# Delta rule, first third: gate columns in split passes, one table set for exponential and logarithm, decays and key products moved

## The reference, cut to what matters

```python
proj = h @ w_in                                   # 4096 columns qkv and z, 8 of b, 8 of a
qkv, z, b_raw, a_raw = split(proj)
qkv = silu(causal_dwconv(qkv, conv_w))            # width 4
q = l2norm(q) * GDN_HEAD_DIM ** -0.5;  k = l2norm(k)
beta = sigmoid(b_raw)
g = -exp(a_log) * softplus(a_raw + dt_bias)       # log decay, per head and token
g = cumsum(g, axis=-1)                            # within a chunk
decay = exp(where(causal, g[..., :, None] - g[..., None, :], -inf))
m = where(strict, einsum("bhnid,bhnjd->bhnij", k * beta, k) * decay, 0.0)
u = triangular_solve(I + m, v * beta)             # and w likewise; then the scan over chunks
```

## Time and profile before

| what | us |
|---|---|
| median of three runs | 1367.81 (1364.25 to 1372.63) |
| profiled execution | 1367.86 |
| its span, first to last instruction | 1366.1 |
| PE busy in the span | 1314.6 (96%) |
| PE from the first matmul of `begin` to the start of tile 13 | 590.80 to 672.03 |
| mean granted TensorE clock | 0.978 of 2.4 GHz |

### The profile page before, as it was taken

How to read it: one execution, slowest core, us unless ns; L and a number is a source line. 1 busy time by engine, 2 the same in 40 slices (tenths; PEclk the granted TensorE clock), 3 DMA queues, 4 the chain that set the end, 5 groups by cost and what they waited for, 6 DMA issues and landing times.

```text
span 1366.1 us, 28690 instructions
## 1 busy us (share of the span) xinstructions
PE 1314.6 (96%) x10343; PEld 1249.7 (91%) x10343; DVE 736.7 (54%) x1539; ACT 706.8 (52%) x1233; POOL 879.3 (64%) x366
## 2 busy tenths in 40 slices
PE   8899989999999999999999999999999999999997
PEld 3589889999989999978989998999999999999996
DVE  4879984321466664254735424655552676555632
ACT  3554445354455555467323224766665555666653
POOL 0454667478859888844222223788888786888794
PEclk9999989999999999998899899999999999999998
DMA  8964436245536555733211211555556554555562
GB/s 336 346 229 161 155 126 210 97 154 183 177 122 205 180 182 169 194 121 110 70 54 63 66 59 64 171 183 181 171 168 188 175 182 154 187 184 179 168 181 74
DMA packets 60837, 217.75 MB, mean 159 GB/s; under 512 B 9832, under 2 KB 11112, under 8 KB 57936
## 3 DMA queue, kind: packets, MB, share of 16 engines
q1 hardware_dynamic: 60752, 216.56, 49.0%
HBM read 215.48 MB, written 1.05 MB: 159 GB/s over the span
## 4 chain that ended last, share of the span: by engine, by line
issue 45%; POOL 38%; PE 15%; ACT 1%; POOLq 1%; DVE 1%; ACTq 0%; DVEq 0%
POOL w_lo L561 38%; PE bank L653 9%; PE bank L732 5%; POOLq L558 0%; ACT h L1410 0%; POOLq L560 0%; ACT w_hi L1410 0%; PE bank L591 0%; PE bank L776 0%; PE bank L592 0%; PE bank L596 0%; ACT bank L1410 0%; DVE bank L3109 0%; POOLq L561 0%; DVE bank L3194 0%
## 5 line engine op out<-in xcount | busy, mean ns | idle before, releaser
L561 POOL TENSOR_TENSOR w_lo<-w_raw,w_hi 128x1024 fp32r<-128x1024 f32 x356 | 876.2, 2472 | 469.6 <-ACT w_hi L1410 468.6
L1410 ACT ACTIVATE w_hi<-w_raw 128x1024 fp32r<-128x1024 f32 x356 | 375.1, 1057 | 142.4 <-PE bank L732 50.6
L653 PE MATMUL bank<-a_hi,w_hi 128*128 128x256 f32 (+4 forms) x1032 | 293.4, 284 | 1.0 <-POOL w_lo L561 1.0
L653 PE MATMUL bank<-a_hi,w_lo 128*128 128x256 f32 (+4 forms) x1032 | 293.0, 284 | 0.0
L653 PE MATMUL bank<-a_lo,w_hi 128*128 128x256 f32 (+4 forms) x1032 | 292.8, 284 | 0.0
L630 PE MATMUL bank<-a_hi,w_hi 128*128 128x256 f32 (+3 forms) x752 | 226.2, 301 | 4.7 <-DVE a_lo L2275 3.9
L630 PE MATMUL bank<-a_lo,w_hi 128*128 128x256 f32 (+3 forms) x752 | 222.4, 296 | 0.0
L630 PE MATMUL bank<-a_hi,w_lo 128*128 128x256 f32 (+3 forms) x752 | 222.1, 295 | 0.0
L653 PEld LDWEIGHTS bank<-a_hi,w_hi 128*128 128x128 f32 x1032 | 195.8, 190 | 1.5 <-POOL w_lo L561 1.2
L653 PEld LDWEIGHTS bank<-a_lo,w_hi 128*128 128x128 f32 x1032 | 195.8, 190 | 0.1
L653 PEld LDWEIGHTS bank<-a_hi,w_lo 128*128 128x128 f32 x1032 | 195.9, 190 | 0.0
(11 more groups left out here) (442 smaller groups left out, 2572.9 us busy)
## 6 DMA issues: line engine op xcount, KB each, us to landing
w_raw<-in_s SPq DMA_DIRECT2D x284, 512.0 KB, 3.5
w_raw<-in_down SPq DMA_DIRECT2D x48, 512.0 KB, 3.5
adaw<-in_w_ada SPq DMA_DIRECT2D x16, 1024.0 KB, 7.4
w_raw<-in_down SPq DMA_DIRECT2D x24, 384.0 KB, 3.1
adab<-in_w_ada_first SPq DMA_DIRECT2D x4, 2048.0 KB, 9.2
ctxt<-in_ctx SPq DMA_DIRECT2D x1, 1024.0 KB, 11.1
x<-in_x SPq DMA_DIRECT2D x1, 1024.0 KB, 17.5
out_h<-h SPq DMA_DIRECT2D x4, 256.0 KB, 2.6
```

The costliest lines, as they stand in the source:

```text
L561: pool.tensor_tensor(w_lo[:, s], w_raw[:, s], w_hi[:, s].bitcast(F32), ALU.subtract) \
L653: ins = mm(banks[bank][:, tk], w_[:, s, k], x_[:, k, tk], start=(m == 0), stop=(m == 3 * KD - 1))
L1410: return nc.scalar.activation(out_, in_, f, **kw)
```

## The change

The gate columns `wba` get a rounded and a low half (ACT, then POOL), and `ba(k)` becomes three fp32r matmuls. ACT preloads the table set that holds exponential and logarithm, and does the gates' absolute value, exponential and logarithm in one run; tanh comes later, under Silu's set. Taps 2 and 3 move behind `rows_ready`; the decay exponentials move from behind the squares of tile 5 to behind `rounded(8)`. DVE runs both key products without taps between them. PE does `y(1, 1)` ahead of fI2. `claimed` waits for each bank of a stage just before the heads that go into it.

```diff
+        wba_hi, wba_lo = (at(f"wba_{n}", [P, KD, 40], where_, F32R) for n, where_ in
+                          (("hi", small_at[0]), ("lo", small_at[0] + 1280)))
...
+        STAGES.remove(("fI2", (6, 7)))
+        STAGES.insert(STAGES.index(("y1.1", (4,))) + 1, ("fI2", (6, 7)))
... POOL
-            remainders(0, UNITS)
+            a_in_ahead = UNIT0["a_in"] + SLOTS
+            remainders(0, a_in_ahead)
+            pool.wait_ge(wba_rounded, 1)
+            pool.tensor_tensor(wba_lo[:], wba[:], wba_hi[:].bitcast(F32), ALU.subtract).then_inc(wba_split, 1)
+            remainders(a_in_ahead, UNITS)
... PE
+            def claimed(name, cols, rows):
+                for (heads, dst), b in zip(heads_in(name, cols, rows), BANKS[name]):
+                    if TURN[name, b]:
+                        pe.wait_ge(taken[b], TURN[name, b])
+                    yield heads, dst
... in broadcast_g, products, by_token, flip, turned, new_values, state_update, w_t, chunk_outputs
-                claim(name)
-                for heads, dst in heads_in(name, cn, cn):
+                for heads, dst in claimed(name, cn, cn):
...
             def ba(k):
-                ins = mm(banks[5][0:40, 0:N2], wba[:, k], h[:, k], start=(k == 0), stop=(k == KD - 1))
+                if k == 0:
+                    pe.wait_ge(wba_split, 1)
+                for m, (w_, x_) in enumerate(((wba_hi, a2_hi), (wba_lo, a2_hi), (wba_hi, a2_lo))):
+                    ins = mm(banks[5][0:40, 0:N2], w_[:, k], x_[:, k, 0:N2], start=(k == 0 and m == 0), stop=(k == KD - 1 and m == 2))
...
             a_in(12, 13)
+            y(1, 1)
             pe.wait_ge(mt_scaled, 4)
             flip("fI2", 2, "uu")
-            y(1, 1)
             y(2, 1)
... ACT
             root(RMS_END, N1, 0)
+            act.wait_ge(gdn_in, 112)
+            fn(wba_hi[:], wba[:], ACT.Copy).then_inc(wba_rounded, 1)
             act.wait_ge(h_in, 16)
...
-            nc.scalar.preload_act_table(ACT.Silu)
+            nc.scalar.preload_act_table_set("natural_log_exp_and_others")
             tap3(0)
-            rounded(0)
...
-            link(fn(tok[:, 0], banks[5][32:32 + HN, 0:N2], ACT.Tanh, scale=0.5))
-            fn(tok[:, 5], banks[5][0:HN, 0:N2], ACT.Abs, bias=hb[:, 1:2]).then_inc(abs_ready, 1)
-            fn(tok[:, 0], tok[:, 0], ACT.Identity, bias=1.0)
+            fn(tok[:, 0], banks[5][32:32 + HN, 0:N2], ACT.Copy)
+            link(fn(tok[:, 5], banks[5][0:HN, 0:N2], ACT.Abs, bias=hb[:, 1:2]))
+            act.sem_inc(abs_ready, 1)
+            link(fn(tok[:, 5], tok[:, 5], ACT.Exp, scale=-1.0))
             fn(hb[:, 2:3], hb[:, 0:1], ACT.Exp)
-            act.wait_ge(abs_ready, 1)
-            link(fn(tok[:, 5], tok[:, 5], ACT.Exp, scale=-1.0))
+            fn(tok[:, 5], tok[:, 5], ACT.Ln, bias=1.0).then_inc(log1p_ready, 1)
+            rounded(0)
             tap3(1)
             rounded(1)
... the copies to halves
-            fn(tok[:, 5], tok[:, 5], ACT.Ln, bias=1.0).then_inc(log1p_ready, 1)
-            tap3(2)
-            rounded(2)
-            nc.scalar.preload_act_table(ACT.Exp)
-            tap3(3)
-            rounded(3)
... the rows of the decays, up to glsp
+            tap3(2)
+            rounded(2)
+            tap3(3)
+            rounded(3)
             nc.scalar.preload_act_table(ACT.Silu)
...
             rounded(4)
+            link(fn(tok[:, 0], tok[:, 0], ACT.Tanh, scale=0.5))
+            fn(tok[:, 0], tok[:, 0], ACT.Identity, bias=1.0)
             prefill(1)
...
             squared(5)
+            tap3(7); rounded(7); activated(6); squared(6); activated(7); squared(7)
+            tap3(8); rounded(8)
             nc.scalar.preload_act_table(ACT.Exp)
             for n, c in enumerate((1, 2, 0)):
                 decay(c, n + 1)
             nc.scalar.preload_act_table(ACT.Silu)
-            tap3(7); rounded(7); activated(6); squared(6)
-            tap3(8); rounded(8); activated(7); squared(7)
...
             rounded(11)
+            flipped("fI1", 1, "tt")
+            product_out(2, 3)
             activated(10)
             squared(10)
-            flipped("fI1", 1, "tt")
-            product_out(2, 3)
... DVE
-            v.tensor_scalar(raw, raw, hb[:, 1:2], 0.0, ALU.add, ALU.max)
-            taps(1)
+            link(v.tensor_scalar(raw, raw, hb[:, 1:2], 0.0, ALU.add, ALU.max))
... the running sum, up to gcum_ready
-            taps(2, 3, 4)
+            taps(1, 2, 3)
... the token columns of rows
             differences(1)
-            taps(5)
+            taps(4, 5)
             differences(2)
...
             key_products(1, 1, 2)
-            taps(10)
             key_products(2, 2, 3)
-            taps(11)
             flipped("fI1", 1, "tt")
-            taps(12)
+            taps(10, 11, 12)
             flipped("fI2", 2, "tt")
```

More of the change, by code:

```diff
@@ L312, in bass_two_blocks @@
             "centre_done conv_seq act_done glu_done g_rounded g_ready")
-        conv_evac, conv4_seq, conv4_act, wba_clear = sems("conv_evac conv4_seq conv4_act wba_clear")
+        conv_evac, conv4_seq, conv4_act, wba_clear, wba_rounded, wba_split = sems(
+            "conv_evac conv4_seq conv4_act wba_clear wba_rounded wba_split")
         abs_ready, log1p_ready, gcum_ready, rows_ready = sems(
@@ L1058, in broadcast_g @@
                 c0, cn = CHUNKS[c]
-                claim(f"g{c}")
-                for heads, dst in heads_in(f"g{c}", cn, cn):
+                for heads, dst in claimed(f"g{c}", cn, cn):
                     for i in range(dst.shape[1]):
@@ L1078, in by_token @@
                 c0, cn = CHUNKS[c]
-                claim(name)
-                for heads, dst in heads_in(name, P, cn):
+                for heads, dst in claimed(name, P, cn):
                     for i in range(dst.shape[1]):
@@ L1139, in turned @@
                     return
-                claim(name)
-                for heads, dst in heads_in(name, GC, GC):
+                for heads, dst in claimed(name, GC, GC):
                     for i in range(4):
@@ L1176, in state_update @@
                 read_out(f"kt{c}")
-                claim(name)
-                for heads, dst in heads_in(name, P, P):
+                for heads, dst in claimed(name, P, P):
                     for i in range(4):
@@ L1188, in w_t @@
                 read_out(f"kt{c}")
-                claim(name)
-                for heads, dst in heads_in(name, cn, P):
+                for heads, dst in claimed(name, cn, P):
                     for i in range(4):
@@ L1848, in _ @@
             squared(5)
+            tap3(7)
+            rounded(7)
+            activated(6)
+            squared(6)
+            activated(7)
+            squared(7)
+            tap3(8)
+            rounded(8)
             nc.scalar.preload_act_table(ACT.Exp)
@@ L1852, in _ @@
             nc.scalar.preload_act_table(ACT.Silu)
[L1853 to L1860, removed]
             tap3(9)
```

1 line of the change is left out of this document (added).

## The result

The changed kernel takes 1357.05 us (median of 6, 1354.67 to 1362.36) where the kernel before takes 1366.94 (median of 6, 1364.25 to 1372.63). The ratio is 0.9922, 95% interval 0.9893 to 0.9950. The profiled execution took 1354.67 with a span of 1352.8. The forecast was 1356.

What follows compares the result with a forecast made beforehand. TensorE alone was taken as the bound, losing 17.9 us to idle time and half clock between `begin` and tile 13. Columns 3.0, waits 3.8 and clock 4.7 gave 11.5 off 1367.86: 1356.4, said as 1356, range 1346 to 1363.

Steps and rivals of the forecast that it cites:

- Gate columns: In `begin`: a step falls from 1.53 to 1.16 us, eight steps save 3.0 us; bounds 0 and 6.1.
- wba_hi and wba_lo: Ahead of `ba(0)`: the copy on ACT and subtraction on POOL cost 0, with 1.1 us of cover.
- Gates: Token rows behind `begin`: ready near 606.5, TensorE comes at 609.3, so the 3.9 us wait goes with 2.8 to spare.
- Squares and decays: At hk: `squared(7)` ends near 626, hk is reached at 629, so the 1.7 us wait goes.
- Key products: From hk to the y pair: new waits 3.9 us in place of 7.7, 2.8 of them at fI2's VectorE half; gain 3.8.
- `claimed`: At kk2's second bank: four heads may start earlier; gain bounded by 0 and 0.8 us, taken as 0.
- Clock: Half-clock stretches between `begin` and tile 13: loss falls from 10.2 to 5.5 us, gain 4.7; bounds 0 and 10.2.
- the clock gives nothing back: Rival: all three half-clock stretches return, gain only 6.8 us, time 1361; chance 0.15.
- it decides: Rival: no half-clock stretch falls, gain 17.0 us, time 1351, or 1347 if the one at 757.37 goes too; chance 0.25.
- The slower rival: From near y(2, 1) up to tile 17 the clock stays low, some 36 us at half, 18 lost: 1370.6; chance 0.06.
- The table set: Rival, in the gate rows: the set does not hold, three loads return, rows 1.1 us late, 1359; chance 0.04.

Runs made afterwards that it cites:

- the run with the gap put back: The changed kernel with the old order of the gates on ACT and DVE (three more table loads, taps 2 and 3 ahead of the rows): 1365.37 us, ratio 0.9981.
- the run with g2 twice: The changed kernel with each of the eight 8-row matmuls of g2 done once more into the same place: 1360.55 us, ratio 0.9946.

## Why the prediction was right, and where it was not

**The sum was right, its split was not.** It had 6.8 us for columns and waits and 4.7 for the clock. On the averages the span is 10.8 us shorter, of which 9.2 ± 0.5 is rest and 1.6 ± 1.1 is loss. That 1356 came so close is luck: one term was 2.4 too small and the other 3.1 too large. Either error alone would have left the time inside the stated range.

*Gate columns.* Predicted 1.16 us a step and 3.0 in all; measured 1.12 to 1.14 and 12.24 - 9.38 = 2.9. Undoing them cost 2.8 without clock. The nearest rows, the fp32r matmuls beside them, were the right price. By the count of four passes in the Trainium skill, FP8 and Floating Point Precision, section TensorE Precision Notes, the gain would have been about 1 (an estimate from that count and the row's 0.59): here the float32 matmul cost 0.59 and 0.22 to its follower, the three split ones 0.37 and 0.12, so about half of the gain is outside the product itself. What the prediction did not say is that this term depends on another: alone, with the gates in their old order, 0.4 of it is spent at once as a longer wait, and no change of the time was measured in two sets, though the rest fell by 2.0 ± 0.4.

*wba_hi and wba_lo.* Cost 0, as predicted, but the cover was thinner: POOL's subtraction took 1.04 us, not 0.75, and ended at 591.27. `ba(0)` came at 592.31, 0.6 later than before, which kept 1.04 of cover; at the old 591.72 it would have been 0.45. The estimate divided a unit's time by its columns, and the measured time of the shorter one is above that share.

*Gates.* Predicted ready near 606.5 and asked for at 609.3; measured 607.04 and 609.73. The wait is gone with 2.7 to spare. The thinnest cover held too, at half its size: unit 4 is subtracted at 603.87 + 2.39 = 606.3, predicted 605.4, and tile 4 starts near 606.7. Undone, this part costs 8.3 us, the most of the three parts that were undone.

*Squares and decays.* No wait at hk, as predicted; it stays away with the gates' order undone and with the products' order undone. That it was this move that took it is by elimination, no run shows it alone.

*Key products.* Predicted 0.3 + 0.3 + 0.5 + 2.8 = 3.9 of waits, measured 0.2 at the first y group and 2.2 at the second, 2.4. The place, the releaser and the cause of the new wait were right, VectorE's chain a little faster than its group means say. The old waits were 7.7 and the 0.3 ahead of the y pair in the earlier trace rows, which the prediction left out of that sum, so like for like 8.0 - 2.4 = 5.6 are gone, not 3.8. That is what the waits at the token rows and at hk had been; the other old waits, 2.4, have made room for 2.4 of new ones. With the key products in their old order the waits come to 1.9, so this part's own order took none away.

*`claimed`.* The prediction put it at 0, bounded by the 0.8 of kk2. It missed a wait further on: in the transposes of `kr` TensorE waited 0.78 us in all four profiles with the old `claim` and waits 0.25 in all ten with `claimed`, whichever other part is undone. That is 0.5 us. No run undoes `claimed` alone, but starting four heads before the second bank is free is what it does. 2.9 + 5.6 + 0.5 = 9.0, which fits the 9.2 of rest.

*Clock.* This is the term that was mis-sized: 4.7 predicted, 1.6 ± 1.1 on the averages. The profiled execution alone seems to say otherwise. In the changed stage 20.5 us at half clock became 6.8, so 3.4 were lost and not 5.5, and the stretch in the g stage that was kept for g2 did not come; behind 740 it lost 6.8 against 5.1. The table of 14 profiles shows what went wrong. The side of the changed kernel was forecast well: 3.4 us at half clock in the g stage and 7.6 near the y pair, where the profiles without the old gap and those with the new wait have 3.4 and 6.3 on the mean. The side of the kernel before was taken from one execution, 20.5 us, with a stretch at 665.21 that seven of the eight profiles without the wait at y(2, 1) do not have; its two profiles and the two with the columns alone have 12.8 on the mean. Half of 12.8 - 9.7 is 1.5, an estimate from few profiles (the two profiles of each kernel alone would give 5.1), but it agrees with the averages. The step that failed is reading the stretches of one execution as what the kernel before always loses. What a kernel sets is an average, 29.3 before and 27.7 after, and one execution scatters about it by some 3 to 4 us.

*Rivals.* That the clock gives nothing back (1361) and that it decides (1351) lie on the two sides of what came. The slower rival did not come: the clock stayed at half through y(2, 1) and kk0 and rose at 661.73, inside tile 13, not 36 us later. The table set held. As for the rule of the Trainium skill, TensorE: Matmul & The Clock Gate, section Why this matters for your kernels, that idle gaps are what to avoid: the run with the gap put back agrees (loss 4.1 more), and the falls at 619.90 in the run with g2 twice and behind g2 of the kernel before had no gap ahead of them, so gaps are not all of it.

## What to carry to other kernels

A part that shortens work ahead of a wait can lose some of its worth in that wait, and a gain of 2 us can vanish in the scatter of the clock: measure it undone in the finished kernel as well as alone, and compare the rest and not only the time. When an idle gap of TensorE is taken away, count the clock behind it too (here it was as much again), and when the new order makes a gap, count the stretch behind that one. Read the clock of both kernels from the mean of many executions or from several profiles: a stretch seen in one profile may be one that most executions don't have. Between a transpose and the product that reads its copy put a tile of other work, and put no taps ahead of the copy.

## What the runs showed of the hardware

- The clock fell inside or right behind runs of 8-row float32 matmuls with TensorE busy throughout: at 619.90 in a run of 32 records, and with the key products' order undone at the end of g1 and right behind g2. Windows on g1 and g2 there and on the stretches that follow, with PE busy for all of them. With such runs halved two profiles have no fall in the g stage, but that few rows are the cause is not shown:

```profile
606.84:608.79 1.95, 1.95 (x18) 1.83 (x18) 0.57 (x5) 1.88 (x4) 1.95 (x2) 1.00 0.71 252
608.79:612.20 3.41, 3.41 (x16) 3.41 (x16) 3.11 (x10) 3.34 (x8) 1.86 (x2) 0.50 0.70 235
613.52:615.61 2.09, 2.09 (x18) 1.97 (x18) 1.09 (x3) 2.06 (x5) 0.45 (x2) 1.00 0.25 67
615.61:619.03 3.42, 3.42 (x16) 3.42 (x17) 2.47 (x9) 1.65 (x4) 2.21 (x1) 0.50 0.39 128
```

- Float32 matmuls that alternate between 8 and 128 stationary rows cost 0.42 us each; in runs of one kind 0.26 (8 rows) and 2.84 / 12 = 0.24 (128 rows, the twelve matmuls of the identity ahead of `begin`).
- A wait of TensorE of 2.2 us came with a half-clock stretch of 3.4 to 6.8 us, in it or just behind it, in six of six profiles, waits of 3.9 to 4.3 us with 6.8 to 13.7 us at half clock up to 640, in five of five. Waits of 1.1 to 1.3 us at fI2, with a second one of 0.3 or 0.8 close behind, came with one in one of five.
- A POOL subtraction of 128x320 took 1.04 us and one of 128x1024 2.35. On the line through both, an estimate from these two, 0.44 us belong to no column.
